# Where the first Fourier step's result is read, and the order of the first loads of the output stage

## The chip, the cores and the metric

The kernel runs on one core of one Trainium2 chip. The metric is the time of one execution on the device in microseconds (us), and lower is better. The profile is one execution recorded by the hardware. In it, PE is the matrix engine (TensorE), DVE the vector engine, ACT the scalar engine, POOL is GpSimd and SP is the engine that issues most of the DMAs.

## What is computed

One layer of a hybrid diffusion backbone, for 4096 grid tokens (64 x 64) and 256 prompt tokens, with width 1024. One input projection feeds four groups of heads (A: neighbourhood attention, B: short convolution, C: Fourier mixing, D: gated linear attention), each is multiplied by its gate, and one output projection merges them. The change is about group C and the output projection:

```python
def fourier_mix(u):
    b, s, w = u.shape
    ug = u.reshape(b, s, N_FOURIER, w // N_FOURIER).astype(jnp.float32)
    f = jnp.fft.fftn(ug, axes=(1, 3), norm='ortho').real
    return f.reshape(b, s, w).astype(u.dtype)
...
    yC = fourier_mix(uC) * jax.nn.silu(gC)
    oD, s_f, s_b = gla_mixer(qD, kD, vD, aF, aB, up_f, b_f, up_b, b_b, s0_f, s0_b, gn_l)
    yD = oD * jax.nn.silu(gD)
    y = jnp.concatenate([yA, yB, yC, yD], axis=-1) @ w_out_l
    return x + gate * y, k, v, s_f, s_b
```

## The kernel before

The program is six stages, one behind the other: modulation, two projection stages (0 and 1), attention with the linear-attention scan, the Fourier stage, and the output stage. Each ends with a wait for its last stores and a barrier of all engines, so nothing of a stage starts before the one ahead of it has ended. Inside a stage every engine runs its own list, written out by hand, and semaphores tie the lists together. There is no scheduler: the order in the code is the order on each engine, and each engine's DMAs go into one queue in that order.

The transform over the 4096 positions is done in two steps of 64. The first runs inside projection stage 1 (`first_step` on PE): for each tile of 128 tokens (two grid columns), real and imaginary results land in `y_sb` (partitions 0 to 63 real, 64 to 127 imaginary), and `send_columns` on SP writes them into the scratch tensor `y1`, 2 x 64 x 64 x 256 numbers, 8.4 MB. The second step is the Fourier stage. SP reads `y1` back in 8 groups of 8 frequencies `k1` (`mid`, 1 MB each, as two DMAs of 64 partitions) and beside each group 256 KB of the table `second`. PE multiplies (L1539, two results of 64 rows side by side), ACT and DVE copy the banks out into one of four buffers `yx`, and ACT stores them into `yc` (L1557, two DMAs of 64 partitions for each group). Group i can be copied out only when the stores of group i - 4 have landed. The prompt's own transform (L1528, tables `whole` and `g` loaded by POOL) stands ahead of all this on PE, and its copy and store (L1546, L1548) ahead of it on ACT.

The attention stage takes 34 tiles of 128 queries (0 to 31 grid, 32 and 33 prompt). In the list of SP tile i begins, when tile i - 1 is done on PE, with the loads for tile i + 1: four of values (L1051), then the scan's (`scan` L1057, `kv` L1059), then queries or keys for a later block; it ends with the stores of tile i (`ya`) and of tile i - 1 (`od`). PE needs the scan's loads of a tile at the end of its first head.

The output stage mixes the four groups (`load_mix`: 9 loads; `combine` on DVE, `join` on POOL, `turn` on PE), splits the mixed tile into a high and a low part (`high` on ACT, `low` on DVE), and multiplies it by the output weights, which come in 8 pieces of 512 KB (`stage_w`, four buffers) and are split in the same way (L1718 on ACT, L1795 on DVE). Pieces 0 to 3 are the weights of the left half of the columns, 4 to 7 of the right. The product of a half waits for its pieces:

```python
for h in range(2):
    pe.wait_ge(gated, t * 2 + h + 1)
    pe.wait_ge(w_lo_done, (h + 1) * len(PIECES) // 2)
    ...
    product(pe, ps_y[s][h][:, :], ...)
    if h == 0:
        prepare_next(turn, t, s)
```

## Time and profile before

| | |
|---|---|
| median of 3 runs | 2787.53 us (2783.85 to 2796.4) |
| profiled execution, its own time | 2787.69 us |
| its span (first to last instruction) | 2786.0 us |
| PE busy | 2554.9 us, 92% of the span |
| DVE, ACT, POOL busy | 45%, 36%, 27% |
| attention stage, last DMAs issued | until 2268.1 us |
| Fourier stage, first DMA | 2270.76 us |
| output stage, first DMA | 2335.51 us |

A busy share is an average over stages. PE is near full in the two projection stages and in most of the output stage, and has almost nothing to do between 2265 and 2368 us, so a gain or loss there shows fully in the time. Times named below are from the start of the span.

### The profile page before, as it was taken

The page shows a single profiled execution, that of the slowest core. Times are in us where ns is not written, and L with a number is a line of the kernel's source. Part 1 is how long each engine was busy: PE and PEld are TensorE (multiplying, and loading weights), DVE is VectorE, ACT ScalarE, POOL GpSimd, SP SyncE. Part 2 cuts the span into 40 slices and gives each one's busy share as a digit, 9 for nine tenths or more (in the row PEclk, how much of TensorE's full clock was granted, in tenths as well). Part 3 has the DMA queues.
Part 4 walks back from the last instruction along what each step waited for, and adds up shares of the span by engine and source line. Part 5 has one row for each costly group of instructions (what it writes and reads, how often), then busy time and mean ns, then how long its engine had stood idle before and what let it go on. Part 6 is the DMA issues. An engine that isn't in the chain of part 4 may idle for free. (4 is left out here: it accounts for less than half of the span.)

```text
span 2786.0 us, 53595 instructions
## 1 busy us (share of the span) xinstructions
PE 2554.9 (92%) x19228; PEld 2056.2 (74%) x19228; DVE 1257.1 (45%) x2620; ACT 990.5 (36%) x2031; POOL 740.5 (27%) x1145
## 2 busy tenths in 40 slices
PE   3899999999999949999999997999899952999999
PEld 1788888888888838888888875777777741888887
DVE  2444343443443343323323325667667722566555
ACT  2444444444444342222222214555555621111110
POOL 2223233233332310000000004333233321444442
PEclk8999999999999979999999998999999976999999
DMA  7433333333333254223223218887677667766664
GB/s 289 144 106 119 110 114 122 102 118 118 107 119 107 84 184 140 93 81 96 92 81 97 92 52 170 179 180 170 144 154 168 153 151 235 244 202 213 209 203 135
DMA packets 271822, 395.35 MB, mean 142 GB/s; under 512 B 43270, under 2 KB 192678, under 8 KB 269628
## 3 DMA queue, kind: packets, MB, share of 16 engines
q1 hardware_dynamic: 258396, 368.21, 46.3%
q10 hardware_dynamic: 12735, 24.07, 2.5%
q8 instruction: 96, 1.57, 0.3%
q0 software_dynamic: 544, 1.09, 0.2%
q14 instruction: 51, 0.41, 0.1%
HBM read 267.31 MB, written 125.96 MB: 141 GB/s over the span
## 5 line engine op out<-in xcount | busy, mean ns | idle before, releaser
L258 PE MATMUL p_ps_m<-p_w_hi,p_h_hi 128*128 128x512 f32 x1904 | 771.8, 405 | 21.1 <-DVE p_h_lo L823 21.1
L260 PE MATMUL p_ps_m<-p_w_hi,p_h_lo 128*128 128x512 f32 x1904 | 750.4, 394 | 0.0
L259 PE MATMUL p_ps_m<-p_w_lo,p_h_hi 128*128 128x512 f32 x1904 | 750.3, 394 | 0.0
L258 PEld LDWEIGHTS p_ps_m<-p_w_hi,p_h_hi 128*128 128x128 f32 x1904 | 359.7, 189 | 99.6 <-issue 21.8
L260 PEld LDWEIGHTS p_ps_m<-p_w_hi,p_h_lo 128*128 128x128 f32 x1904 | 358.9, 189 | 80.7
L259 PEld LDWEIGHTS p_ps_m<-p_w_lo,p_h_hi 128*128 128x128 f32 x1904 | 360.1, 189 | 73.3
L258 PE MATMUL o_ps_y<-o_w_hi,o_y_hi 128*128 128x512 f32 x544 | 217.5, 400 | 9.7 <-DVE o_y_lo L1784 9.7
L260 PE MATMUL o_ps_y<-o_w_hi,o_y_lo 128*128 128x512 f32 x544 | 217.4, 400 | 0.0
L259 PE MATMUL o_ps_y<-o_w_lo,o_y_hi 128*128 128x512 f32 x544 | 215.7, 397 | 0.0
L537 POOL TENSOR_TENSOR p_ve<-p_ss,p_eps 128x1 f32<-128x1 f32 x68 | 12.9, 190 | 601.1 <-ACT p_xr L603 601.1
L814 DVE TENSOR_TENSOR p_xt<-p_xt,p_ps_r 128x1024 f32<-128x1024 f32 x68 | 82.7, 1216 | 193.0 <-PE p_ps_r L714 193.0
L577 POOL TENSOR_TENSOR p_la<-p_la,p_cum 128x512 f32<-128x512 f32 x34 | 44.0, 1295 | 426.7 <-ACT p_cum L616 426.7
L817 DVE TENSOR_SCALAR p_xt<-p_xt,mod 128x128 f32<-128x128 f32 x544 | 146.1, 342 | 2.5
L1463 DVE COPY a_p_t<-a_ps_t 128x512 f32<-128x512 f32 (+1 forms) x136 | 91.6, 674 | 117.0 <-PE a_ps_t L1309 117.0
L1710 ACT ACTIVATE o_y_hi<-o_ps_t 128x512 fp32r<-128x512 f32 x68 | 36.9, 596 | 257.5 <-PE o_ps_t L1739 257.5
L823 DVE TENSOR_TENSOR p_h_lo<-p_xt,p_h_hi 128x1024 fp32r<-128x1024 f32 x68 | 83.3, 1225 | 98.7 <-ACT p_h_hi L608 98.7
L258 PEld LDWEIGHTS o_ps_y<-o_w_hi,o_y_hi 128*128 128x128 f32 x544 | 102.9, 189 | 33.3 <-issue 10.1
L259 PEld LDWEIGHTS o_ps_y<-o_w_lo,o_y_hi 128*128 128x128 f32 x544 | 102.8, 189 | 24.9
L260 PEld LDWEIGHTS o_ps_y<-o_w_hi,o_y_lo 128*128 128x128 f32 x544 | 102.7, 189 | 23.8
L1345 PEld LDWEIGHTS a_ps_o<-a_v_win,a_p_t 128*64 128x64 f32 x2112 | 75.3, 140 | 57.9 <-issue 41.2
L1345 PE MATMUL a_ps_o<-a_cv,a_p_t 128*64 128x64 f32 x2048 | 92.0, 226 | 23.5 <-DMA a_kv<-s_kv 16.1
L1414 DVE TENSOR_REDUCE a_max_c<-a_ps_c 128x1 f32<-128x512 f32 x128 | 88.0, 687 | 47.4 <-PE a_ps_c L1288 46.1
(217 smaller groups left out, 4512.6 us busy)
## 6 DMA issues: line engine op xcount, KB each, us to landing
a_scan<-s_scan SPq DMA_DIRECT2D x68, 258.0 KB, 5.7
s_scan<-p_w_raw SPq DMA_DIRECT2D x136, 128.0 KB, 2.4
a_kv<-s_kv SPq DMA_DIRECT2D x68, 256.0 KB, 6.3
a_v_win<-s_p SPq DMA_DIRECT2D x132, 128.0 KB
p_xr<-in_x_sample SPq DMA_DIRECT2D x32, 512.0 KB, 4.0
p_xt<-in_x_sample_t SPq DMA_DIRECT2D x32, 512.0 KB, 4.7
p_xr<-in_x_columns SPq DMA_DIRECT2D x32, 512.0 KB, 10.1
p_xt<-in_x_columns_t SPq DMA_DIRECT2D x32, 512.0 KB, 10.8
```

The costliest lines, as they stand in the source:

```text
L258: pe.matmul(out, left_hi(k), right_hi(k), start=(k == 0), stop=False)
L259: pe.matmul(out, left_hi(k), right_lo(k), start=False, stop=False)
L260: last = pe.matmul(out, left_lo(k), right_hi(k), start=False, stop=(k == K8 - 1))
L537: pool.tensor_tensor(ve[s][:, :], ss[s][:, :], eps[:, 0:1], ALU.add).then_inc(ve_done, 1)
L577: pool.tensor_tensor(la[:, :, :], la[:, :, :], cum[:, :, :], ALU.subtract).then_inc(la_done, 1)
L814: dve.tensor_tensor(xt[s][:, :, :], xt[s][:, :, :], ps_r[:, s, :].unsqueeze(1).broadcast_to([P, K8, P]), ALU.mult).then_inc(normed, 1)
L817: last = dve.tensor_scalar(xt[s][:, k, :], xt[s][:, k, :], keep["mod"][:, 1, k, j:j + 1], keep["mod"][:, 0, k, j:j + 1], ALU.mult, ALU.add)
L823: dve.tensor_tensor(h_lo[s][:, :, :], xt[s][:, :, :], h_hi[s][:, :, :], ALU.subtract).then_inc(lo_done, 1)
L1345: last = pe.matmul(ps_o[z * HD:z * HD + HD, at:at + HD], p_t[p][:, m * P + z * HD:m * P + z * HD + HD], val, start=(n == 0), stop=(n == le ...
L1414: dve.tensor_reduce(max_c[:, p:p + 1], ps_c[p][:, :], AX.X, ALU.max).then_inc(maxc_done, 1)
L1463: dve.tensor_copy(p_t[p][:, 0:cols], ps_t[0][:, 0:cols]).then_inc(t0_sb, 1)
L1710: act.activation(y_hi[s][:, 4 * b:4 * b + 4, :], ps_t[b][:, :, :], ACT.Copy).then_inc(hi_done, 1)
```

## The change

Five edits.

1. `y1` is laid out by group: (8, 2, 64, 8, 256), so that a group of 8 frequencies is one block of 1 MB. `send_columns` issues four DMAs for each tile in place of two.
2. The table `second` (2 MB) and the first four groups of `mid` (4 MB) have buffers that live through the attention and the Fourier stage. SP loads the groups there in tiles 26 to 29 and the table in tile 30, behind the stores of the tile.
3. The Fourier stage loads groups 4 to 7 alone, each in one DMA of 128 partitions.
4. The prompt's transform stands behind the groups on PE and on ACT.
5. In the output stage SP loads the input of tile 0, weight pieces 0 to 3, the input of tile 1, then pieces 4 to 7; the split of the pieces on ACT and DVE is put in the matching order; `taps` and `gn` go to ACT's queue.

```diff
             def send_columns(t, s):
                 sp.wait_ge(y_done, t + 1)
                 for r in range(2):
-                    sp.dma_start(io["y1"][r, bass.ds(2 * t, 2)].rearrange("b k c -> k b c"), y_sb[s][64 * r:64 * r + 64, :, :]).then_inc(y_sent[s], 16)
+                    for z in range(2):
+                        sp.dma_start(io["y1"][:, r, bass.ds(2 * t, 2)][:, z], y_sb[s][64 * r:64 * r + 64, z, :]).then_inc(y_sent[s], 16)
...
-                            act.wait_ge(y_sent[1 - s], (t - 2) * 16 + (1 - s) * -16 + 16)
+                            act.wait_ge(y_sent[1 - s], (t - 2 + s) * 32)
...
+                if isinstance(i, int) and 26 <= i < 30:
+                    g = i - 26
+                    sp.dma_start(fourier["mid"][:, 8 * g:8 * g + 8, :], io["y1"][g].rearrange("r b q c -> (r b) q c")).then_inc(fourier_in, 16)
+                if isinstance(i, int) and i == 30:
+                    sp.dma_start(fourier["second"][:, :, :], io["dft_second"]).then_inc(fourier_in, 16)
...
-            for i in range(GROUPS):
-                for r in range(2):
-                    sp.dma_start(mid[64 * r:64 * r + 64, 8 * i:8 * i + 8, :], io["y1"][r, :, 8 * i:8 * i + 8, :]).then_inc(group_in[i], 16)
-                sp.dma_start(second[:, 8 * i:8 * i + 8, :], io["dft_second"][:, 8 * i:8 * i + 8, :]).then_inc(group_in[i], 16)
+            for i in range(GROUPS // 2, GROUPS):
+                at = 8 * i - 32
+                sp.dma_start(mid[1][:, at:at + 8, :], io["y1"][i].rearrange("r b q c -> (r b) q c")).then_inc(group_in[i], 16)
...
+            for n in range(2 * GROUPS):
+                if n % 2 == 0 and n >= GROUPS:
+                    pe.wait_ge(group_in[n // 2], 16)
+                if n >= BANKS:
+                    pe.wait_ge(freed[n % 2], (n - BANKS) // 2 + 1)
+                ...
             pe.wait_ge(gp_in, 64)
...
-            load_mix(1, 1)
-            sp.dma_start(taps[:, :, :].rearrange("p a c -> p (a c)"),
-                         io["conv_w"].rearrange("a t c -> a (t c)").broadcast_to([P, 3 * W_GRP])).then_inc(taps_in, 16)
...
+            load_mix(0, 0)
+            load_weights(range(4))
+            load_mix(1, 1)
+            load_weights(range(4, 8))
...
             square(0, 0)
+            split_high(range(2))
+            high(0, 0, 0)
+            split_high(range(2, 4))
             square(1, 1)
+            split_high(range(4, 8))
...
             combine(0, 0)
+            split_low(range(2))
+            low(0, 0, 0)
+            split_low(range(2, 4))
             combine(1, 1)
+            split_low(range(4, 8))
```

Three places show how the lists move. The first is SP in the attention stage, at the end of tile 26 and in the loads for tile 28 (`s_y` is the scratch tensor `y1`, `s_p` holds the values). Before:

```order
L1031 DMA a_k_lo<-s_qk_lo 128x2x960
L1116 DMA s_ya<-a_o_sb 8x16x256
L1121 DMA s_od<-a_od_sb 128x256 x2
L1051 DMA a_v_win<-s_p 128x1x256 x4
L1057 DMA a_scan<-s_scan 64x1032
L1059 DMA a_kv_0<-s_kv 64x2x512
```

Of the change:

```order
L1033 DMA a_k_lo<-s_qk_lo 128x2x960
L1118 DMA s_ya<-a_o_sb 8x16x256
L1123 DMA s_od<-a_od_sb 128x256 x2
L1126 DMA f_mid<-s_y 128x2048
L1053 DMA a_v_win<-s_p 128x1x256 x4
L1059 DMA a_scan<-s_scan 64x1032
L1061 DMA a_kv_0<-s_kv 64x2x512
```

One DMA of 1 MB stands ahead of all loads for tile 28, and in the same way in the next three tiles; in tile 30 it is the table of 2 MB.

The second is SP at the start of the output stage. Before:

```order
L1636 DMA o_u<-s_conv_u 128x256 x3
L1641 DMA o_taps<-in_conv_w 128x768
L1646 DMA o_stage_w<-in_w_out 128x2x512 x8
L1649 DMA o_gate<-s_mod 128x1024 x2
```

Of the change (its two stretches of inputs end with the `o_u` rows):

```order
L1643 DMA o_u<-s_conv_u 128x256 x3
L1650 DMA o_stage_w<-in_w_out 128x2x512 x4
L1636 DMA o_ya<-s_ya 128x256
...
L1643 DMA o_u<-s_conv_u 128x256 x3
L1650 DMA o_stage_w<-in_w_out 128x2x512 x4
L1658 DMA o_gate<-s_mod 128x1024 x2
```

`taps` has left SP's list, and four weight pieces have moved ahead of the input of tile 1.

The third is DVE at the same place, before:

```order
L1778 TENSOR_TENSOR o_o_n<-o_o,o_r 128x256
L1769 TENSOR_TENSOR o_o<-o_od 128x256
L1771 TENSOR_TENSOR o_u_w<-o_u,o_taps 128x768
L1773 TENSOR_REDUCE o_ss<-o_o_sq 128x4
L1776 TENSOR_REDUCE o_conv<-o_u_w 128x256
L1778 TENSOR_TENSOR o_o_n<-o_o,o_r 128x256
L1795 TENSOR_TENSOR o_w_lo<-o_stage_w,o_w_hi 128x2x512 x4
L1784 TENSOR_TENSOR o_y_lo<-o_ps_t,o_y_hi 128x512 x2
L1795 TENSOR_TENSOR o_w_lo<-o_stage_w,o_w_hi 128x2x512 x4
```

Of the change:

```order
L1795 TENSOR_TENSOR o_o_n<-o_o,o_r 128x256
L1809 TENSOR_TENSOR o_w_lo<-o_stage_w,o_w_hi 128x2x512 x2
L1801 TENSOR_TENSOR o_y_lo<-o_ps_t,o_y_hi 128x512 x2
L1809 TENSOR_TENSOR o_w_lo<-o_stage_w,o_w_hi 128x2x512 x2
L1786 TENSOR_TENSOR o_o<-o_od 128x256
L1788 TENSOR_TENSOR o_u_w<-o_u,o_taps 128x768
L1790 TENSOR_REDUCE o_ss<-o_o_sq 128x4
L1793 TENSOR_REDUCE o_conv<-o_u_w 128x256
L1795 TENSOR_TENSOR o_o_n<-o_o,o_r 128x256
L1809 TENSOR_TENSOR o_w_lo<-o_stage_w,o_w_hi 128x2x512 x4
```

The whole `combine` of tile 1 (five operations) has moved from ahead of the first four pieces to behind them, and now stands ahead of the last four.

## Rows read from the trace of the kernel before

**Rows 1.** The page's first line.

```profile
span 2786.0 us, 53595 instructions
```

**Rows 2.** Chain of work that ended last (start us, us, what).

```profile
2344.42 6.87 DMA o_taps<-in_conv_w
...
2400.68 0.87 PE o_ps_t L1739 x8
...
2412.76 0.87 PE o_ps_t L1739 x8
```

**Rows 3.** Windows of the Fourier stage: PE, PEld, DVE, ACT, POOL, PEclk, DMA share, GB/s.

```profile
2271.00:2288.00 17.00, 0.00 (x0) 0.00 (x0) 0.00 (x0) 0.00 (x0) 2.98 (x4) 0.50 0.97 224
2313.00:2334.00 21.00, 9.44 (x48) 4.55 (x48) 2.77 (x4) 2.39 (x4) 0.00 (x0) 0.71 0.83 269
```

**Rows 4.** DMA view of 2265 to 2336 us: packets; issues, KB each, us to landing.

```profile
DMA packets 5271, 16.53 MB, mean 233 GB/s; under 512 B 1312, under 2 KB 1941, under 8 KB 4245
...
f_mid<-s_y SPq DMA_DIRECT2D x16, 512.0 KB, 22.1
s_yc<-f_yx ACTq DMA_DIRECT2D x16, 256.0 KB, 12.4
```

**Rows 5.** Timeline of the Fourier stage (start, us, engine, line; idle before and releaser).

```profile
2270.76 1.16 SPq L1510 DMA_DIRECT2D f_mid<-s_y  x2
...
2288.57 6.56 PE L1528 MATMUL f_psp<-f_gp,f_whole 128*128 128x256 f32 x16 [23.32 <-DMA f_whole<-in_dft_whole]
...
2313.62 0.60 ACT L1544 ACTIVATE f_yx<-f_ps 128x512 f32<-128x512 f32 x1 [10.34 <-DMA s_yc<-f_yx]
...
2315.13 3.47 PE L1539 MATMUL f_ps<-f_mid,f_second 128*64 128x256 f32 x16 [3.40 <-DMA f_second<-in_dft_second]
...
2327.37 2.63 PE L1539 MATMUL f_ps<-f_mid,f_second 128*64 128x256 f32 x16 [2.76 <-DMA f_second<-in_dft_second]
...
2335.51 0.34 SPq L1638 DMA_DIRECT2D o_gn<-in_gla_norm_g  x1
```

**Rows 6.** Windows with DMAs of 64 and of 128 partitions, columns as in rows 3.

```profile
2172.00:2174.00 2.00, 2.00 (x34) 1.73 (x30) 1.52 (x7) 1.12 (x3) 0.00 (x0) 1.00 1.12 199
2375.00:2377.00 2.00, 2.00 (x15) 1.74 (x14) 0.00 (x0) 0.56 (x2) 0.00 (x0) 1.00 1.07 391
```

**Rows 7.** Attention: SP issues and PE tile ends in the timeline.

```profile
2165.24 3.86 SPq L1051 DMA_DIRECT2D a_v_win<-s_p  x4
...
2171.64 0.60 SPq L1059 DMA_DIRECT2D a_kv<-s_kv  x1
...
2178.72 1.10 PE L1373 MATMUL a_ps_g<-a_kv,a_scan 128*64 128x64 f32 x32
...
2240.74 1.13 PE L1373 MATMUL a_ps_g<-a_kv,a_scan 128*64 128x64 f32 x32
```

**Rows 8.** Attention windows behind two bursts of loads, columns as in rows 3.

```profile
2176.00:2178.00 2.00, 1.90 (x20) 1.17 (x20) 1.80 (x6) 1.82 (x4) 2.00 (x5) 1.00 0.42 99
2236.00:2238.00 2.00, 1.77 (x36) 1.52 (x37) 1.33 (x5) 1.30 (x4) 1.23 (x2) 1.00 0.03 9
```

**Rows 9.** The stores of `y1`: their issues; waits of SP in projection stage 1.

```profile
L438 SPq DMA_DIRECT2D s_y<-p_y_sb x64: 612/630/670, 1055.4 to 1644.0; - x64
...
SPq L438 <- ACT p_y_sb L693: 209.6, 22, 11.1
```

**Rows 10.** Timeline of the output stage's start, as in rows 5.

```profile
2343.47 0.72 POOL L1672 TENSOR_TENSOR o_mix<-o_ya,o_g_ad 128x256 f32<-128x256 f32 x1 [7.82 <-DMA o_u<-s_conv_u]
...
2354.38 0.94 DVE L1778 TENSOR_TENSOR o_o_n<-o_o,o_r 128x256 f32<-128x256 f32 x1 [0.50 <-POOL o_r L1680]
...
2361.24 5.15 DVE L1795 TENSOR_TENSOR o_w_lo<-o_stage_w,o_w_hi 128x1024 fp32r<-128x1024 f32 x4
...
2367.86 0.77 PE L258 MATMUL o_ps_y<-o_w_hi,o_y_hi 128*128 128x512 f32 x1 [9.71 <-DVE o_y_lo L1784]
...
2375.80 1.03 PE L1739 MATMUL o_ps_t<-ident,o_mix 128*128 128x128 f32 x8
...
2382.12 0.69 DVE L1807 TENSOR_TENSOR o_gx<-o_ps_y,o_gate 128x512 f32<-128x512 f32 x1 [3.77 <-DMA o_x<-in_x_sample]
...
2388.38 1.09 PE L1739 MATMUL o_ps_t<-ident,o_mix 128*128 128x128 f32 x8 [0.35 <-POOL o_mix L1685]
```

More of the change, by code:

```diff
@@ L1484, in fourier_stage @@
         sem = lambda name: new_sem("f_" + name)
-        second = sb("second", [P, 64, 64])
-        mid = sb("mid", [P, 64, W_GRP])
+        second = early["second"]
+        mid = [early["mid"], sb("mid1", [P, 32, W_GRP])]
         yx = [sb(f"yx{s}", [P, 4, W_GRP]) for s in range(SLOTS)]
@@ L1523, in _ @@
         def _(pe):
+            for n in range(2 * GROUPS):
[3 more added lines that the diff above has]
+                    pe.wait_ge(freed[n % 2], (n - BANKS) // 2 + 1)
+                for j in range(2):
+                    for z in range(2):
+                        k1 = 8 * (n // 2) + 4 * z + n % 2 * 2 + j
+                        last = pe.matmul(ps[n % BANKS][64 * z:64 * z + 64, j, :], second[:, k1, :], mid[k1 // 32][:, k1 % 32, :], start=True, stop=True)
+                last.then_inc(filled, 1)
             pe.wait_ge(gp_in, 64)
@@ L1530, in _ @@
             last.then_inc(yp_mm, 1)
-            for n in range(2 * GROUPS):
-                if n % 2 == 0:
-                    pe.wait_ge(group_in[n // 2], 48)
-                if n >= BANKS:
-                    pe.wait_ge(freed[n % 2], (n - BANKS) // 2 + 1)
-                for j in range(2):
-                    for z in range(2):
-                        k1 = 8 * (n // 2) + 4 * z + n % 2 * 2 + j
-                        last = pe.matmul(ps[n % BANKS][64 * z:64 * z + 64, j, :], second[:, k1, :], mid[:, k1, :], start=True, stop=True)
-                last.then_inc(filled, 1)
         @block.scalar
@@ L1694, in _ @@
         def _(act):
+            act.dma_start(taps[:, :, :].rearrange("p a c -> p (a c)"),
+                          io["conv_w"].rearrange("a t c -> a (t c)").broadcast_to([P, 3 * W_GRP])).then_inc(taps_in, 16)
+            act.dma_start(gn[:, :], io["gla_norm_g"].broadcast_to([P, HD])).then_inc(gn_in, 16)
             for s in range(2):
@@ L1710, in high, with split_high @@
                     act.activation(y_hi[s][:, 4 * b:4 * b + 4, :], ps_t[b][:, :, :], ACT.Copy).then_inc(hi_done, 1)
+            def split_high(which):
+                for n in which:
+                    h, m = PIECES[n]
+                    act.wait_ge(w_in[n % 4], 16 * (n // 4 + 1))
+                    act.activation(w_hi[:, 2 * m:2 * m + 2, 512 * h:512 * h + 512], stage_w[n % 4][:, :, :], ACT.Copy).then_inc(w_hi_done, 1)
             square(0, 0)
+            split_high(range(2))
+            high(0, 0, 0)
+            split_high(range(2, 4))
             square(1, 1)
-            for n, (h, m) in enumerate(PIECES):
-                if n == len(PIECES) // 2:
-                    high(0, 0, 0)
-                act.wait_ge(w_in[n % 4], 16 * (n // 4 + 1))
-                act.activation(w_hi[:, 2 * m:2 * m + 2, 512 * h:512 * h + 512], stage_w[n % 4][:, :, :], ACT.Copy).then_inc(w_hi_done, 1)
+            split_high(range(4, 8))
             for t, s, j in tile_pairs(act):
@@ L1785, in low, with split_low @@
                                       ALU.subtract).then_inc(lo_done, 1)
+            def split_low(which):
+                for n in which:
+                    h, m = PIECES[n]
+                    part = slice(2 * m, 2 * m + 2), slice(512 * h, 512 * h + 512)
+                    dve.wait_ge(w_hi_done, n + 1)
+                    dve.tensor_tensor(w_lo[:, part[0], part[1]], stage_w[n % 4][:, :, :], w_hi[:, part[0], part[1]],
+                                      ALU.subtract).then_inc(w_lo_done, 1)
             dve.wait_ge(taps_in, 16)
             combine(0, 0)
+            split_low(range(2))
+            low(0, 0, 0)
+            split_low(range(2, 4))
             combine(1, 1)
[L1790 to L1796 removed]
+            split_low(range(4, 8))
             dve.wait_ge(small_in, 32)
@@ L1824, in build @@
             projection_stage(nc, io, keep, 1, early)
-            attention_scan_stage(nc, io, keep, early)
-        fourier_stage(nc, io, keep)
+            fourier = {"second": inner.enter_context(nc.sbuf_tensor("f_second", [P, 64, 64], F32)),
+                       "mid": inner.enter_context(nc.sbuf_tensor("f_mid0", [P, 32, W_GRP], F32))}
+            attention_scan_stage(nc, io, keep, early, fourier)
+            fourier_stage(nc, io, keep, fourier)
         output_stage(nc, io, keep)
```

40 lines of the change are left out of this document (18 added, 22 removed).

## The prediction

> **What bounds the kernel now.** I read the page first, then the stretches in which PE has little to do. The span is 2786.0 us [rows 1]; the same execution took 2787.69 us, so 1.7 us lie outside it, and the median of the runs is 2787.53, so the sum can be made against 2787.7. The chain of waits shows that the end is set by PE through the output stage, at one tile each 12.08 us (2412.76 - 2400.68) [rows 2], and before that by DMAs and by the preparation of the output stage. Two stretches are therefore worth their full length: the Fourier stage, 64.75 us (2270.76 to 2335.51), in which PE is only fed by loads [rows 5], and the 32.35 us from there to the first output product at 2367.86 [rows 10].
>
> In the Fourier stage the DMA engines are the bound. While nothing but loads run they are busy 0.97 and move 224 GB/s, later with stores mixed in 269 GB/s [rows 3]. Over the whole stretch 16.53 MB move at 233 GB/s [rows 4]. PE waits 23.32 us for the prompt's table, then for each group again; the last group comes at 2327.37, and the stage ends 8.1 us behind it [rows 5].
>
> In the output stage the inputs of tile 0 are there at 2343.47 (POOL starts on them), but DVE needs `taps`, which stands behind the inputs of tile 1 on SP and lands 6.87 us after its issue at 2344.42, at 2351.3 [rows 2, 10]. Then DVE does both combines, four weight pieces (5.15 us from 2361.24) and the low part, and the first product starts [rows 10].
>
> **The change, part by part.**
>
> *Stores of y1.* Two more issues for each of 32 tiles, at 0.63 us each [rows 9]: 1.3 us of SP for a tile. SP stands waiting for ACT at this very store, 209.6 us over 22 tiles, 9.5 each [rows 9], so the cover is there and I cost it at 0. Were the cover gone it would be 32 x 1.3 = 40 us. The reader of the buffer's semaphore comes two tiles later.
>
> The Trainium skill's page "DMA: Bandwidth & Descriptors", section "Why a DMA increments its semaphore by 16 and not by 1", says that a DMA uses the largest number of engines up to 16 that divides the outermost size on both sides; the new store has 8 groups outermost in memory, so by that rule it runs on 8 engines, not 16. By the rule 64 KB would take about twice as long, still far less than two tiles; it changes no term, but it speaks against this layout and is part of the rival that ends slower.
>
> *Loads in the attention stage.* 1 MB in each of tiles 26 to 29, 2.1 MB in tile 30, ahead of the loads for the tile after next. The nearest rates are 199 GB/s in a burst of DMAs of 64 partitions and 391 GB/s where all have 128 [rows 6]: 1.05 MB takes 2.7 to 5.3 us, 2.1 MB takes 5.4 to 10.5 us. What is behind them: the values and scan loads, issued from 2165.24 to 2172.2 [rows 7]. They have landed by about 2176.5: the DMA share has fallen to 0.42 in the window from 2176 [rows 8]. PE ends its tile at 2178.72 + 1.1 and wants the scan's inputs some 3 us into the next, about 2183. The slack is 6 us, more than 5.3, so 0 for these four tiles. For the 2.1 MB: in the window from 2236 the loads are done (share 0.03) [rows 8], the tile ends at 2240.74 + 1.1 [rows 7], need about 2245: slack 8.5 to 9 against 5.4 to 10.5. I put 1 us on the path, with 0 below and 8 above (an excess of 1.5 in each of five tiles).
>
> *Fourier stage.* Of its loads, 4.2 MB of `mid` and 2.1 MB of table go. Left are 4.19 MB of `mid` (4 DMAs), 1.05 MB for the prompt, 4.19 MB of stores and 0.26 MB of the prompt's result: 9.7 MB of 16.0. The rate is the unknown. Bounds: at the 233 GB/s of before it takes 41.6 us [rows 4], at the 391 of full DMAs 24.8 us [rows 6]. The loads are now 128 partitions each, the stores still 64, so I take the middle, 310 to 330: 30 us. Two things are added to that. At the front PE can start at once from the buffers, but the store of group 0 cannot be issued before one group (3.47 us slow clock [rows 5]) and its copy; loads fill that time, so 1.5 us for the first packet only. At the end, behind the last load, stand the group's product (2.63), now the prompt's product (6.56 at the granted clock of 0.5, half of it at full clock; taken 5), then its copy (0.6), issue (0.4), landing and barrier: before, from the last group to the next stage was 8.1 us [rows 5]; now it is 8.1 + 5 = 13, of which 4.5 are stores that count in the 30. So 1.5 + 30 + 8.5 = 40 us, against 64.75: **-25 us**. With the bounds of the rate: 24.8 + 10 = 35 (-30), 41.6 + 10 = 52 (-13). The wait for a free `yx` slot, 10.34 us before [rows 5], lies inside this: stores can only be made when the engines serve them.
>
> The Trainium skill's page "SBUF — State Buffer", section "Can I just issue two DMAs to hit both halves?", says no: only one transfer over all 128 partitions reaches all ports, and two halves serialize. The trace agrees with its sign (199 against 391 [rows 6]). By that rule alone the loads would run at the full rate, and the stage would lie near the 35 us end.
>
> *Output stage.* From its start S, in the steps of before. Inputs of tile 0 are in at S + 7.6 (before: 2343.47 - 2335.51 = 8.0, with `gn` ahead). `taps` comes on ACT's queue with the first issues and is there. DVE's combine took 4.0 us (2351.3 to 2355.3) [rows 10]; POOL's own three products now run beside it and not ahead, +0.5: S + 12.1. Then two pieces at 1.29 (5.15 / 4): S + 14.7. `turn` (2 us slow) starts at S + 13, ACT's high parts end by S + 15.5, DVE's low parts by S + 16.2. Two more pieces: S + 19. The four pieces are 2.1 MB, issued by S + 6.2 and landed by about S + 14 at 300 GB/s, in time. **The first product starts at S + 19 in place of S + 32.35.** But the second product needs all 8 pieces, and DVE stands with the combine of tile 1 (4.3) and four pieces (5.15) ahead: S + 19 + 9.5 = S + 28.5. PE is at that point itself at S + 19 + 7.9 (2375.80 - 2367.86) + 1 = S + 28, so it waits 0.5. Before, the second product started at 2376.8, S + 41.3. Gain there: 41.3 - 28.5 = 12.8. What is late next: `x` of tile 0. Before it came at 2382.12, just in time (PE waited 0.35 at 2388.38 for the mix of tile 2 that hangs on it) [rows 10]. It is still behind pieces, gates and the inputs of tile 2 on SP; the gap between the last piece and `x` stays about 10 us, which makes it some 1 us later against PE. **-12 us**, bounds -14 (no wait at all) and -3 (the last four pieces, which now wait for a buffer to be split before they can be issued, land late and only the `taps` wait is gone in part).
>
> **Sum:** 2787.7 + 0 + 1 - 25 - 12 = **2752 us** (2751.7).
>
> **Rivals.**
> - *Only bytes are saved, not rate:* the Fourier stage runs on at 233 GB/s and takes 52 us. For it: DMA share was 0.97 with 224 GB/s [rows 3]. Against it: 391 GB/s with full DMAs [rows 6]. 2787.7 + 1 - 13 - 12 = 2764.
> - *Full rate and no late `x`:* Fourier -30, output -14: 2745. For it: the same 391. Against it: stores of 64 partitions share the engines.
> - *The attention stage pays:* each of the five extra loads stalls PE by 3 us, the rest as forecast: 2787.7 + 15 - 37 = 2766. Against it: 6 us of slack in [rows 7, 8]. In favour: landing is read from a share in windows of 2 us.
> - *The split order fails:* the second product waits for pieces 4 to 7, the output stage gains 3, the rest as forecast: 2761.
> - *Slower:* the stores of `y1`, four per tile with 8 separate blocks in memory, land so late that ACT's copy of the result waits for its buffer and PE behind it. The tile there is about 19 us (the 9.5 of waiting are half of it), the buffer is free for two tiles, so a store would have to take over 35 us; from there each further us costs 32 us in half the tiles' pairs, 16 or so in all. It decides from 37 us on path: a landing of 38 us, for 2787.7 - 36 + 48 = 2800. Nothing in [rows 9] supports it.
>
> **How the numbers follow.** A difference under 0.5% (14 us) can't be told from none here. Chances: forecast 0.45; bytes only 0.15; full rate 0.18; attention pays 0.09; split order 0.08; slower 0.02; the remaining 0.03 for something unseen of which most would leave the time within 0.5%. The range from 2739 to 2767 takes in the first five. Faster: 0.95; within 0.5%: 0.03; slower: 0.02.
>
> **What would show it.** Right: the Fourier stage's PE work begins within 1 us of its start, its windows show over 300 GB/s, and it lasts about 40 us; the tile ends of PE in the attention stage stay 15 to 16 us apart in tiles 27 to 31; the first output product comes at S + 19, the second half at S + 28 to 29. Wrong: a wait of PE for `kv` or `scan` in tiles 28 to 32, a wait for a `yx` slot that outlasts the loads, a first output product late because of the weight loads, or a tile in projection stage 1 that is longer than before.

## The result, and the profile after

The changed kernel takes 2751.24 us (median of 4 runs, 2742.02 to 2755.03), the kernel before 2786.98 us on the same chip: a ratio of 0.9865, with a 95% interval of 0.9839 to 0.9891. The forecast was 2752. The profiled execution took 2755.03 us with a span of 2753.3, 32.7 less than the 2786.0 of before [rows 1]. Read by stages, from the first DMA of one to the first DMA of the next:

| | before | after | difference | forecast |
|---|---|---|---|---|
| start to the Fourier stage | 2270.76 | 2282.43 | +11.7 | +1 |
| Fourier stage | 64.75 | 29.88 | -34.9 | -25 |
| output stage | 450.5 | 441.0 | -9.5 | -12 |
| span | 2786.0 | 2753.3 | -32.7 | -36 |

So the total came out, and none of its three stage terms did. The timeline of the changed kernel's Fourier stage (start, us, engine, line; idle before and releaser):

```profile
2282.43 2.24 SPq L1518 DMA_DIRECT2D f_mid<-s_y  x4
2282.46 13.29 PE L1539 MATMUL f_ps<-f_mid,f_second 128*64 128x256 f32 x96 [5.62 <-PEq L81]
...
2297.30 1.95 PE L1539 MATMUL f_ps<-f_mid,f_second 128*64 128x256 f32 x16 [1.55 <-DMA f_mid<-s_y]
2298.56 0.60 ACT L1551 ACTIVATE f_yx<-f_ps 128x512 f32<-128x512 f32 x1 [5.33 <-DMA s_yc<-f_yx]
2301.33 3.42 PE L1539 MATMUL f_ps<-f_mid,f_second 128*64 128x256 f32 x16 [2.08 <-DMA f_mid<-s_y]
2304.68 3.88 PE L1545 MATMUL f_psp<-f_gp,f_whole 128*128 128x256 f32 x16
2309.23 0.42 ACTq L1564 DMA_DIRECT2D s_yc<-f_yp  x1
2312.31 0.33 SPq L1636 DMA_DIRECT2D o_ya<-s_ya  x1
```

The 23.32 us in which PE waited for the prompt's table [rows 5] are gone: PE starts with the stage, waits 3.6 us in all for its last two groups, and the last one is there 18.9 us behind the stage's start (2301.33 - 2282.43) in place of 56.6. The wait for a free `yx` slot is 5.33 us, not 10.34 [rows 5]. The DMA view of the stage, and behind it windows (columns as in rows 3, in the order of this sentence) of the middle of the stage and of two places in the attention stage:

```profile
DMA packets 2449, 9.72 MB, mean 313 GB/s; under 512 B 400, under 2 KB 656, under 8 KB 1936
...
f_mid<-s_y SPq DMA_DIRECT2D x4, 1024.0 KB, 8.4
s_yc<-f_yx ACTq DMA_DIRECT2D x16, 256.0 KB, 7.4
```

```profile
2286.00:2302.00 16.00, 12.37 (x104) 8.00 (x102) 3.62 (x6) 2.56 (x5) 0.00 (x0) 0.93 1.01 400
2252.00:2254.00 2.00, 0.89 (x18) 0.69 (x20) 1.67 (x4) 0.26 (x2) 0.00 (x0) 0.96 0.90 230
2254.00:2256.00 2.00, 2.00 (x31) 1.56 (x27) 0.00 (x0) 0.50 (x3) 0.00 (x0) 0.50 1.04 213
```

At the same DMA share (1.01 against 0.97) the engines now move 400 GB/s where they moved 224 [rows 3]. The last two windows belong to the attention stage: there the granted clock falls from 0.96 to 0.50, which is 1.2 of 2.4 GHz, behind a window in which PE was busy 0.89 of 2 us. In the attention stage's timeline, SP's issues in tile 26, and then ends of tiles and waits on PE:

```profile
2167.18 0.45 SPq L1126 DMA_DIRECT2D f_mid<-s_y  x1
2167.74 4.78 SPq L1053 DMA_DIRECT2D a_v_win<-s_p  x4
...
2176.77 0.60 SPq L1061 DMA_DIRECT2D a_kv<-s_kv  x1
...
2181.45 1.10 PE L1381 MATMUL a_ps_g<-a_kv,a_scan 128*64 128x64 f32 x32
2186.11 0.34 PE L1353 MATMUL a_ps_o<-a_cv,a_p_t 128*64 128x64 f32 x4 [0.61 <-DMA a_kv<-s_kv]
2202.58 0.34 PE L1353 MATMUL a_ps_o<-a_cv,a_p_t 128*64 128x64 f32 x4 [0.66 <-DMA a_kv<-s_kv]
2219.29 0.34 PE L1353 MATMUL a_ps_o<-a_cv,a_p_t 128*64 128x64 f32 x4 [0.90 <-DMA a_kv<-s_kv]
...
2247.02 0.75 PE L1381 MATMUL a_ps_g<-a_kv,a_scan 128*64 128x64 f32 x18
...
2274.86 1.98 PE L1381 MATMUL a_ps_g<-a_kv,a_scan 128*64 128x64 f32 x32 [0.54 <-DVE a_s_at L1451]
```

The four tiles from 2178.72 to 2240.74 [rows 7] took 62.0 us; from 2181.45 to 2247.02 they take 65.6, with a wait for the scan's `kv` in each of three of them that no tile in the profile of before has. These waits add up to 2.2 us of the 3.6 (1.2 of 2.9 in changed_again); PE's own work is 0.9 us longer, the rest lies in small gaps, and neither was followed further. The last two take 27.8 us, not 22.5. On SP the loads behind the new one are stretched: the values' four issues take 4.78 us, not 3.86, and from the first of them to the last `kv` it is 9.0 us (2176.77 - 2167.74) where it was 6.4 (2171.64 - 2165.24) [rows 7]. Between 2150 and 2240 us a load of `kv` takes 9.5 us from issue to landing (median), 6.2 before. The start of the output stage:

```profile
2321.92 0.43 DVE L1786 TENSOR_TENSOR o_o<-o_od 128x256 f32<-128x256 f32 x1 [16.43 <-DMA o_u<-s_conv_u]
2326.33 0.94 DVE L1795 TENSOR_TENSOR o_o_n<-o_o,o_r 128x256 f32<-128x256 f32 x1 [1.31 <-POOL o_r L1689]
2327.20 2.88 DVE L1809 TENSOR_TENSOR o_w_lo<-o_stage_w,o_w_hi 128x1024 fp32r<-128x1024 f32 x2
...
2335.26 0.76 PE L258 MATMUL o_ps_y<-o_w_hi,o_y_hi 128*128 128x512 f32 x1 [4.25 <-DVE o_w_lo L1809]
2338.94 5.17 DVE L1809 TENSOR_TENSOR o_w_lo<-o_stage_w,o_w_hi 128x1024 fp32r<-128x1024 f32 x4
2344.25 0.47 PE L258 MATMUL o_ps_y<-o_w_hi,o_y_hi 128*128 128x512 f32 x1 [0.49 <-DVE o_w_lo L1809]
```

From the stage's start S = 2312.31 the inputs of tile 0 are in at S + 9.6, the first product starts at S + 22.95 and the second at S + 31.9, which before was S + 41.3. The 9.4 us between these are the stage's gain.

### The profile page after: what moved, and what is told of

Its sections match the earlier page's. It is cut to its first block and busy times, and to the rows that moved or that the text cites. A ratio compares the mean times of both kernels' runs of the same rounds, so it can differ in the third digit from the quotient of the medians.

```text
span 2753.3 us, 53748 instructions
## 1 busy us (share of the span) xinstructions
PE 2558.0 (93%) x19228; PEld 2060.3 (75%) x19228; DVE 1256.9 (46%) x2620; ACT 989.7 (36%) x2031; POOL 740.0 (27%) x1145
## 5 line engine op out<-in xcount | busy, mean ns | idle before, releaser
L258 PE MATMUL p_ps_m<-p_w_hi,p_h_hi 128*128 128x512 f32 x1904 | 771.6, 405 | 20.5 <-DVE p_h_lo L824 20.4
L260 PEld LDWEIGHTS o_ps_y<-o_w_hi,o_y_lo 128*128 128x128 f32 x544 | 102.6, 189 | 23.8
## 6 DMA issues: line engine op xcount, KB each, us to landing
p_xr<-in_x_columns SPq DMA_DIRECT2D x32, 512.0 KB, 10.2
```

The costliest lines, as they stand in the source:

```text
L258: pe.matmul(out, left_hi(k), right_hi(k), start=(k == 0), stop=False)
L260: last = pe.matmul(out, left_lo(k), right_hi(k), start=False, stop=(k == K8 - 1))
```

## The experiments

The theory after this reading: the loads of the Fourier stage became fast because they span 128 partitions, not because of the new layout; the early loads cost the attention stage more than forecast because they meet its own loads. All ratios below are to the kernel before on the same chip. A summary by stage, in us, from the profile of each kernel ("four tiles" and "last two" are the attention tiles named above):

| kernel | median | ratio (95%) | four tiles | last two | Fourier | output |
|---|---|---|---|---|---|---|
| before | | | 62.0 | 22.5 | 64.75 | 450.5 |
| changed | 2751.24 | 0.9865 (0.9839-0.9891) | 65.6 | 27.8 | 29.88 | 441.0 |
| changed_again | 2743.58 | 0.9849 (0.9827-0.9870) | 64.9 | 25.7 | 29.61 | 441.6 |
| no_early | 2758.89 | 0.9907 (0.9884-0.9929) | 62.0 | 22.5 | 50.08 | 441.6 |
| half_loads | 2749.63 | 0.9875 (0.9852-0.9899) | 65.2 | 27.8 | 37.24 | 441.2 |
| old_layout | 2745.44 | 0.9861 (0.9840-0.9882) | 65.3 | 28.0 | 29.78 | 441.3 |
| one_dma | 2766.77 | 0.9935 (0.9914-0.9956) | 62.1 | 26.1 | 44.58 | 449.9 |
| late_issue | 2750.91 | 0.9879 (0.9859-0.9900) | 71.6 | 25.5 | 29.63 | 442.3 |
| last_tiles | 2740.74 | 0.9841 (0.9819-0.9863) | 62.1 | 26.1 | 29.48 | 441.4 |
| prompt_first | 2759.59 | 0.9915 (0.9888-0.9943) | 65.5 | 26.1 | 41.34 | 441.5 |
| out_only | 2774.12 | 0.9968 (0.9950-0.9985) | 62.1 | 26.0 | 62.88 | 441.4 |
| taps_only | 2784.83 | 0.9993 (0.9978-1.0009) | 62.1 | 22.5 | 63.84 | 446.4 |
| taps_behind | 2744.57 | 0.9864 (0.9842-0.9886) | 62.1 | 22.5 | 29.56 | 441.9 |
| best | 2741.42 | 0.9843 (0.9823-0.9864) | 62.1 | 22.5 | 29.28 | 441.3 |

**changed_again**: the changed kernel with no edit.

> The changed kernel once more, unchanged, as the measure of how far two profiles and two medians of one kernel lie apart. Theory: Fourier stage 29.9 us and output stage 441.0 us within 0.5 us of the first profile, a median within 3 us of 2751; the tiles 26 to 33 of the attention stage together again 8 to 13 us longer than the 127.1 to 129.3 us of the kernels without early loads. Rival, that the 10 us are chance of one profile (clock dips): 130 us or less this time.

The Fourier stage repeats to 0.3 us and the output stage to 0.6; the four tiles are long again. From the end of tile 25 to the Fourier stage it is 132.0 us this time, not 137.0: less than the 8 to 13 us extra that was expected, and not down to the 130 of the rival, though one_dma, with nothing loaded early, has 131.5. So this total alone doesn't decide it; the four tiles do. The median is 7.7 us lower, more than the 3 that were expected. What differs lies ahead of the change: the row that ends tile 25 stands at 2145.4 us in the first profile of the changed kernel and at 2136.9 in this one, and in the fourteen profiles of this study, whose code up to there is the same but for the stores of `y1`, anywhere from 2134.6 to 2145.4. A difference of a few us between two medians is therefore decided by stages here, not by totals.

**no_early**: nothing is loaded in the attention stage.

```diff
...
-            for i in range(GROUPS // 2, GROUPS):
-                at = 8 * i - 32
-                sp.dma_start(mid[1][:, at:at + 8, :], ...)
+            for i in range(GROUPS):
+                at = 8 * i % 32
+                sp.dma_start(mid[i // 4][:, at:at + 8, :], ...)
+                sp.dma_start(second[:, 8 * i:8 * i + 8, :], io["dft_second"][:, 8 * i:8 * i + 8, :]).then_inc(group_in[i], 16)
```

> The changed kernel with nothing loaded in the attention stage: all eight groups of the first step's result (one DMA of 128 partitions each) and the table (eight pieces) are loaded in the Fourier stage. Theory, that DMAs of 128 partitions over contiguous blocks run at about 400 GB/s: the stage moves 16 MB, 12 of them loads, and takes 48 to 52 us (64.75 before, 29.9 in the changed kernel); the attention stage goes back to its length of before (-11 us); total near 2764, 0.992 of before. Rival, that only the bytes moved out of the stage helped and the rate stays that of before (233 GB/s, some 270 at best): the stage takes 60 us or more, total 2774 or more.

50.1 us, as the theory has it. The same 16 MB that took 62.9 to 64.75 us now take 50.1, and the attention stage is as long as before (62.0 and 22.5). So of the 34.9 us, 14.7 are there with no byte moved out of the stage (with the new place of the prompt's product, which costs some of it: see one_dma), and the bytes moved out give 20.2 (there the prompt's new place helps: see prompt_first).

**half_loads**: the four late groups as two DMAs each.

```diff
-                sp.dma_start(mid[1][:, at:at + 8, :], io["y1"][i].rearrange("r b q c -> (r b) q c")).then_inc(group_in[i], 16)
+                for r in range(2):
+                    sp.dma_start(mid[1][64 * r:64 * r + 64, at:at + 8, :], io["y1"][i][r]).then_inc(group_in[i], 16)
```

> The changed kernel, but the four groups that are loaded in the Fourier stage come as two DMAs of 64 partitions each, from the same contiguous blocks of 1 MB. Theory, that the number of partitions sets the rate: the 4.2 MB come at about 210 GB/s in place of 400, the last group is 6 to 9 us later, and the stage takes 36 to 39 us in place of 29.9; total +6 to +9. Rival, that the contiguous block made the loads fast: within 2 us of 29.9.

37.2 us, 7.4 more, from contiguous blocks. A window of 16 us in the middle of the stage:

```profile
2270.00:2286.00 16.00, 11.62 (x84) 7.55 (x82) 2.77 (x4) 2.39 (x4) 1.50 (x3) 0.82 1.02 261
```

The engines are busy at 1.02 and move 261 GB/s, against 400 in the changed kernel. A DMA of 64 partitions is also half as large, 512 KB, but the size is not what slows it. In the changed kernel's output stage weight pieces of 512 KB over 128 partitions, with inputs of 128 and 256 KB around them, move at 404 GB/s:

```profile
2320.00:2326.00 6.00, 0.00 (x0) 0.00 (x0) 3.10 (x4) 2.53 (x3) 3.95 (x5) 0.50 1.06 404
```

The median does not show the 7.4 us (2749.63, between the two medians of the changed kernel); it is less than those differ by.

**old_layout**: the changed kernel with `y1` as before, two stores for each tile; only the loads differ from before, and they span 128 partitions.

```diff
-                    for z in range(2):
-                        sp.dma_start(io["y1"][:, r, bass.ds(2 * t, 2)][:, z], y_sb[s][64 * r:64 * r + 64, z, :]).then_inc(y_sent[s], 16)
+                    sp.dma_start(io["y1"][r, bass.ds(2 * t, 2)].rearrange("b k c -> k b c"), y_sb[s][64 * r:64 * r + 64, :, :]).then_inc(y_sent[s], 16)
...
-                sp.dma_start(mid[1][:, at:at + 8, :], io["y1"][i].rearrange(...
+                sp.dma_start(mid[1][:, at:at + 8, :], io["y1"][:, :, 8 * i:8 * i + 8, :].rearrange(...
```

> The changed kernel with the result of the first step stored as in the kernel before (its old shape, two stores for each tile, not four), and each group still loaded by one DMA of 128 partitions, which now reads runs of 8 KB a partition out of 128 places 64 KB apart and not one block of 1 MB. Theory, that the number of partitions sets the rate and the block layout does nothing: Fourier stage within 1 us of 29.7, total within 3 us of the changed kernel. Rival, that the contiguous megabyte in memory is what made the loads fast: the stage is 5 us or more longer.

29.78 us: the theory again. A window of 16 us in it:

```profile
2276.00:2292.00 16.00, 11.41 (x104) 7.60 (x102) 3.72 (x6) 2.66 (x5) 0.19 (x1) 1.00 1.01 406
```

406 GB/s from 8 KB runs that lie 64 KB apart: the block of 1 MB does nothing for the time.

**one_dma**: the kernel before, one line (and the count that PE waits for).

```diff
-                for r in range(2):
-                    sp.dma_start(mid[64 * r:64 * r + 64, 8 * i:8 * i + 8, :], io["y1"][r, :, 8 * i:8 * i + 8, :]).then_inc(group_in[i], 16)
+                sp.dma_start(mid[:, 8 * i:8 * i + 8, :], io["y1"][:, :, 8 * i:8 * i + 8, :].rearrange("r b q c -> (r b) q c")).then_inc(group_in[i], 16)
```

> The kernel before, with the two DMAs of 64 partitions for each group made into one of 128, from the same places of the old layout, and nothing else. Theory (partitions set the rate): the Fourier stage falls from 64.75 (62.9 and 63.8 in two other traces of the same code) to 50 to 54 us, as in the kernel with nothing loaded early (50.1), plus what the prompt's product ahead of the groups costs; total near 2776. Rival (layout sets the rate): within 2 us of 63.

44.58 us, 18.3 to 20.2 less than in the three profiles with two DMAs, and better than expected. A window of 16 us in its Fourier stage, and PE there:

```profile
2278.00:2294.00 16.00, 7.16 (x20) 5.45 (x22) 0.00 (x0) 0.36 (x1) 0.00 (x0) 0.53 1.01 403
```

```profile
2286.84 6.76 PE L1527 MATMUL f_psp<-f_gp,f_whole 128*128 128x256 f32 x16 [18.38 <-DMA f_whole<-in_dft_whole]
2293.53 12.51 PE L1538 MATMUL f_ps<-f_mid,f_second 128*64 128x256 f32 x112
2309.64 3.28 PE L1538 MATMUL f_ps<-f_mid,f_second 128*64 128x256 f32 x16 [3.59 <-DMA f_second<-in_dft_second]
```

Seven groups run through behind the prompt's product without a wait, and the stage ends 8.9 us behind the last one. With the prompt's product last (no_early) the stage takes 5.5 us longer for the same bytes (no_early has the new layout too, which by old_layout does nothing): there PE waits for its first group anyway, and the prompt's product stands exposed at the end.

**prompt_first**: the changed kernel with the prompt's product, copy and store ahead of the groups.

> The changed kernel, but PE and ACT do the prompt's transform ahead of the eight groups again, as before. Theory: PE can't use the buffers filled in the attention stage until the prompt's table has landed (21.8 to 23.3 us in the traces of before, estimated at 10 to 16 with 4.2 MB of other loads in place of 12.6); the first stores of yc leave that much later and come in a crowd, so the stage takes 38 to 42 us in place of 29.9, total +8 to +12. Rival, that the engines are busy with loads in that time anyway and the stage stays bound by its 9.7 MB: within 3 us of 29.9.

41.34 us, as the theory has it. PE waits for the prompt's table 19.81 us and then runs all eight groups in one piece:

```profile
2288.75 6.09 PE L1535 MATMUL f_psp<-f_gp,f_whole 128*128 128x256 f32 x16 [19.81 <-DMA f_whole<-in_dft_whole]
2294.77 14.03 PE L1546 MATMUL f_ps<-f_mid,f_second 128*64 128x256 f32 x128
```

Some 5.6 us of this wait lie ahead of the stage; from its start (2274.54) the table is there at 14.2 us, at 17.8 before. The median is 16 us above that of changed_again on the same chip, of which 4 are the longer attention stage of this profile. So the edit that puts the prompt last is worth 11.6 us when half of the groups lie ready, and costs 5.5 when none do.

**late_issue**: the early loads are issued behind the loads for the next tile.

```diff
+                if isinstance(i, int) and 26 <= i < 30:
+                    ...
                 sp.wait_ge(o_done, 4 * i + 5)
...
-                if isinstance(i, int) and 26 <= i < 30:
-                    ...
```

> The changed kernel, but each of the five early loads is issued behind its tile's own loads (values, scan, queries, keys, bias), not ahead of them. Theory, that the attention stage lost its 10 us because the extra bytes stood ahead of the values and scan inputs in the queue: tiles 27 to 32 go back to 15.6 us, PE's waits for the keys-and-values of the scan are gone, and the attention stage gets 5 to 10 us back, total 2741 to 2746. Rival, that the bytes cost the same wherever they stand (the engines are loaded, or the clock falls anyway): no more than 2 us from the changed kernel, and the Fourier stage may begin with a wait for the table.

The theory on the order in the queue falls: the four tiles take 71.6 us, longer still, and the median is that of the changed kernel. The worst wait, and the windows behind it:

```profile
2182.74 0.34 PE L1353 MATMUL a_ps_o<-a_cv,a_p_t 128*64 128x64 f32 x4 [3.23 <-DMA a_kv<-s_kv]
```

```profile
2180.00:2182.00 2.00, 0.00 (x0) 0.00 (x0) 0.33 (x3) 0.00 (x0) 0.00 (x0) 1.00 0.77 220
2182.00:2184.00 2.00, 1.26 (x22) 1.19 (x24) 0.00 (x0) 0.87 (x3) 1.01 (x2) 0.74 0.26 101
2184.00:2186.00 2.00, 2.00 (x25) 1.88 (x22) 0.00 (x0) 0.11 (x2) 1.06 (x2) 0.50 0.26 88
```

The early groups now take 13.6 us (median) to land, 6.9 in the changed kernel: they share the engines with the tile's own loads and with those of the next tile. Which of the two makes `kv` late was not taken apart. PE does nothing for these 3.23 us, the granted clock then falls to 0.50, and the tile takes 20.4 us.

**last_tiles**: all five early loads in tile 32, behind its own loads.

```diff
-                if isinstance(i, int) and 26 <= i < 30:
-                    g = i - 26
-                    ...
-                if isinstance(i, int) and i == 30:
+                if isinstance(i, int) and i == 32:
+                    for g in range(4):
+                        sp.dma_start(fourier["mid"][:, 8 * g:8 * g + 8, :], ...)
                     sp.dma_start(fourier["second"][:, :, :], io["dft_second"]).then_inc(fourier_in, 16)
```

> The changed kernel, but all five early loads (6.3 MB) are issued in tile 32, behind the last loads that the attention stage needs itself. In the trace of the kernel before the DMA engines stand nearly idle from there to the stage's end, 2250 to 2270. Theory, that the early loads cost the attention stage time because they meet its own loads, in whatever order: tiles 26 to 31 go back to 15.2 to 15.8 us each, no wait for keys-and-values of the scan, from the start of tile 26's end (the row of the scan's result ahead of it) to the Fourier stage 127 to 130 us in place of 137; the 6.3 MB need 16 us at 391 GB/s and are in before the stage ends; total near 2742. Rival, that the stage's tail then waits for these loads or that the stores of the last tiles are held up by them: the stage is as long as in the changed kernel or longer, total 2750 or more.

The four tiles are at 62.1 again with no wait for `kv`, and from the end of tile 25 to the Fourier stage it is 129.6 us, against 137.0 and 132.0 in the two profiles of the changed kernel. Windows of the attention stage's end:

```profile
2246.00:2260.00 14.00, 12.33 (x140) 9.34 (x136) 4.43 (x13) 2.90 (x10) 3.84 (x6) 0.51 1.01 419
2260.00:2268.00 8.00, 1.97 (x32) 1.79 (x32) 0.42 (x1) 0.91 (x2) 0.01 (x1) 0.50 0.36 119
```

6.3 MB go through a stretch in which the engines stood idle before, at 419 GB/s beside PE's work, and are in ahead of the stage's end. They are not free there. The table, last in the queue, takes 18.0 us to land, and the tiles' stores of `od` stand behind it. In this profile the last tile is slow by itself (14.8 us at the low clock) and covers that. In the next two kernels with the same loads (taps_behind, then best) the last tile takes 11.3 us, and ACT's last copy waits for such a store:

```profile
2262.62 0.60 ACT L1253 ACTIVATE a_od_sb<-a_ps_g 128x512 f32<-128x512 f32 x1 [5.08 <-DMA s_od<-a_od_sb]
2268.16 0.60 ACT L1253 ACTIVATE a_od_sb<-a_ps_g 128x512 f32<-128x512 f32 x1 [6.33 <-DMA s_od<-a_od_sb]
```

From the row that ends the last tile to the Fourier stage it is then 10.4 and 11.0 us, against 7.5 to 7.6 in all others. From the end of tile 27 to the Fourier stage the three kernels with the loads in tile 32 take 95.0 to 95.7 us, the five with nothing early 92.0 (three, with 22.5 in the last two tiles) or 95.6 to 95.7 (two, with the clock fallen), and the five with loads ahead of their tiles' own 98.2 to 101.0. So the new place costs some 3 us where the clock holds, and the old one 2.4 to 6 more. The median is 2.8 us below changed_again on the same chip, with intervals of the ratios that overlap (0.9819 to 0.9863 and 0.9827 to 0.9870): the gain is shown in the stage, not in the total.

**out_only**: the kernel before with the output stage of the changed one.

> The kernel before with only the output stage of the changed kernel (taps on ACT's queue, weight pieces in two halves between the inputs of two tiles, new order of the splits). If that stage's gain is its own: -9.5 us as read between the two traces, total 2777, 0.9965 of before, all stages ahead of it unchanged. Rival, that part of the 9.5 came from a different state of the queues at the stage's start (the stores of the Fourier stage and the prompt's store end closer to it now): -12 to -13, since the inputs of tile 0 then land at 7.6 us and not 9.6 us behind the stage's start.

The output stage takes 441.4 us, -9.1: its gain is its own, and the first expectation holds. The inputs of tile 0 land 10.2 us behind the stage's start, here too.

**taps_only**: the kernel before with `taps` and `gn` on ACT's queue, weight pieces and splits as before.

> The kernel before with only the loads of taps and norm weights moved to ACT's queue; weight pieces and splits stay as they were. Theory, that most of the output stage's gain is the wait for taps that is gone: the combine starts 7.5 to 8.5 us behind the stage's start in place of 15.8, and the stage gets 5 to 8 us shorter, total near 2780. Rival, that the order of the splits is what counts and the eight pieces (landed last) set the second product anyway: 0 to 3 us.

-4.1 us, between the two. The combine begins 10.3 us behind the start and not at 8, so the taps are no longer waited for but cost the inputs behind them. The order of the pieces and splits is the other 5.0 us (446.4 to 441.4).

**taps_behind**: last_tiles, with `taps` on SP behind the inputs of tile 0.

```diff
             load_mix(0, 0)
+            sp.dma_start(taps[:, :, :]...).then_inc(taps_in, 16)
             load_weights(range(4))
...
                 dve.wait_ge(conv_done, t + 1)
+                if isinstance(t, int) and t == 0:
+                    dve.wait_ge(taps_in, 16)
```

> The kernel with all early loads in tile 32, and in the output stage taps issued on SP behind the inputs of tile 0 and ahead of the weight pieces, not as the first issue of ACT's queue; DVE waits for taps only ahead of the product that reads them. In all six traces in which taps stands first the combine begins 9.6 to 10.3 us behind the stage's start, with POOL at 8.0 before. Theory, that the 384 KB of taps ahead of tile 0's inputs delay these by about 2 us: POOL and DVE's first operation begin at 7.8 to 8.3 us, taps land at 9.5 to 10.5, and the first product comes at 22 to 23.5 in place of 23.3, the stage is 0 to 1.5 us shorter than 441.4. Rival, that the weight pieces behind are what slows the inputs: 9.6 us or later again.

The stage begins at 2297.73. Its timeline:

```profile
2306.14 0.42 DVE L1785 TENSOR_TENSOR o_o<-o_od 128x256 f32<-128x256 f32 x1 [16.02 <-DMA o_u<-s_conv_u]
2308.37 0.96 DVE L1789 TENSOR_TENSOR o_u_w<-o_u,o_taps 128x768 f32<-128x768 f32 x1 [1.81 <-DMA o_taps<-in_conv_w]
...
2317.67 1.54 POOL L1682 TENSOR_TENSOR o_mix<-o_ya,o_g_ad 128x256 f32<-128x256 f32 x1 [3.90 <-DMA o_u<-s_conv_u]
```

The inputs are in at 8.4 us, not 9.6 to 10.3, so `taps` ahead of them is what delays them. Nothing is won by it: the product with `taps` starts at 10.6, the first output product at 22.7 (23.3 in last_tiles), and the inputs of tile 1, now 3.90 us late for POOL, take it back. The stage is 0.4 us longer.

**best**: last_tiles, with the prompt's product ahead of the last group.

```diff
             for n in range(2 * GROUPS):
+                if n == 2 * GROUPS - 2:
+                    pe.wait_ge(gp_in, 64)
+                    ...
                 if n % 2 == 0 and n >= GROUPS:
```

The line that is left out is the prompt's product; ACT copies and stores it ahead of the last group too.

> The kernel with all early loads in tile 32, and the prompt's product moved from behind the last group to ahead of it, into PE's wait for that group (0.82 and 2.33 us ahead of the last two groups in the trace of that kernel). Theory: the prompt's copy and store no longer stand behind the last group's, so the Fourier stage takes 27 to 28.5 us in place of 29.5, total near 2739, 0.983 of before. Rival, that the prompt's table has not landed by then or that ACT, which waits for the prompt's product, frees the buffers of the last groups later: 29.5 us or more.

29.28 us, no gain of size: the rival holds, the table lands only 17.35 us behind the stage's start.

```profile
2291.07 3.72 PE L1536 MATMUL f_psp<-f_gp,f_whole 128*128 128x256 f32 x16 [1.70 <-DMA f_whole<-in_dft_whole]
```

PE waits for it and the last group waits behind it. No version stands clearly apart from last_tiles.

## Why the prediction came out

**Stores of y1: 0, right.** From the first to the last of these stores it is 589.9 and 590.0 us in the two profiles of the changed kernel, 588.6 in those of before and of old_layout, and the 1.3 us are the two more issues of the last tile alone. old_layout takes the two more away again and is within 3 us of the changed kernel's second median. How long such a store takes to land no row here shows, so the rule of the Trainium skill's page "DMA: Bandwidth & Descriptors", section "Why a DMA increments its semaphore by 16 and not by 1", stays unchecked; the rival that ended slower did not come.

**Attention: +1 forecast, +11.7 read, some 6 of it from the change.** The step that failed is "the slack is 6 us, more than 5.3, so 0 for these four tiles". The landing was read from a DMA share of 0.42 in a window of 2 us, and the transfer was taken as the only thing the new load costs. In fact the loads behind it are issued over 9.0 us, not 6.4, and a `kv` takes 9.5 us to land, not 6.2: counted from the end of tile 26, the last `kv` is issued 12.5 us behind it, not 8.7 (2176.77 - 2164.27 and 2171.64 - 2162.92), and lands 3.3 us later still. That is 7.1 us against the 6 of slack, and 2176.77 + 9.5 = 2186.3 is where PE's first wait for it ends (2186.11). The forecast added only the 5.3 us of the transfer at its worst and called the slack enough. A wait for `kv` appears in tiles where none was; I had named it as what would show me wrong. (One profile without early loads, out_only, has such a wait too, 0.87 us in tile 27; none of the eight has one in the four tiles.) In the five profiles with early loads in tiles 26 to 30 ahead of the tiles' own the four tiles take 64.9 to 65.6 us, in the eight without them 62.0 to 62.1: 3.2 us on average. The last two tiles take 25.7 to 28.0 with them (five) and 22.5 to 26.1 without (eight): that is where the granted clock falls, and it falls ahead of the last tile (25.7 us or more) in all five of the first kind and in three of the eight of the other. On average it is 3.2 us more (27.1 against 23.8). So 6.4 us is the reading for the change, of which the half in the last two tiles is the weaker one: it rests on how often the clock falls, in thirteen profiles. Of the 11.7, the pair of profiles has 8.9 in these six tiles, 1.7 by the end of tile 25 and 1.0 in tiles 26 and 27, these last two figures no more than the spread of profiles of one code. The 6.4 is inside the bound of 8 that I gave, whose "excess of 1.5 in each of five tiles" is close to the truth in sum; I took the wrong end.

**Fourier stage: -25 forecast, -34.9 read.** Right were the rate's direction, the immediate start of PE and the choice of 128 partitions as the cause. Mis-sized were two terms. The rate while loads run is 400 GB/s, not 310 to 330: stores of 64 partitions among loads of 128 do not pull it down to the middle. The tail was forecast at 13 us behind the last load, with 4.5 of it stores; it is 11.0. And I put all 9.7 MB ahead of the tail but for those 4.5 us, though loads are not queued behind stores: from the start to the last load it was to be 1.5 + 25.5 = 27 us and it is 18.9. 27 + 13 = 40; 18.9 + 11.0 = 29.9. The lower bound of 35 us, which had the full rate but the same tail arithmetic, was no bound. Seen over the whole stage, tail and all, the mean is 325 GB/s (9.72 MB in 29.88 us), the very middle that I took: the 30 us were right for the whole stage, and the 10 us beside them were too much. The slow bound was misread as well. The 233 GB/s [rows 4] are the mean of a window of 71 us, 6 of them outside the stage; over the stage itself it was 247 GB/s, which makes the 41.6 us 39.3. And PE is not quite as idle around it as the text ahead of the prediction has it: between 2265 and 2368 us it was busy 29.1 of 103 us, with work that stood behind loads.

The rule of the Trainium skill's page "SBUF — State Buffer", section "Can I just issue two DMAs to hit both halves?", that only one transfer over 128 partitions reaches all ports, is what half_loads, old_layout and one_dma test, and they agree with it: 261 against 400 and 406 GB/s. By that rule alone the stage lay near my bound; I should have taken it, since the nearest row of before said the same [rows 6]. The prediction named this and still took the middle.

**Output stage: -12 forecast, -9.5 read.** The order of events is the one forecast, with x late as named (DVE waits 3.99 us for it, nothing hangs on that). The step that failed is "inputs of tile 0 are in at S + 7.6", with `taps` "there" at no cost: its 384 KB go first and the inputs come at S + 9.6 to 10.3 in all eleven profiles with `taps` first. taps_behind shows the cause. The combine also takes 5.3 us, not 4.5: with POOL at work beside it the product with `taps` takes 1.48 us, not 0.95, and the last step waits 1.31 us for POOL's `o_r`, not 0.50. The first product is 4.0 us later than forecast (2.0 for the inputs, 0.8 for the combine, the rest in the splits and the low part), the second 3.4, and 12.8 - 3.4 is 9.4.

**The sum.** +10.7, -9.9 and +2.5 against the terms as forecast leave +3.3 us in the profile, less than the 7.7 by which two medians of the changed kernel differ. That the total fell on the forecast is luck: the attention stage cost more than forecast by about as much as the Fourier stage gained more. "The attention stage pays" (in part, some 6 us and not 15) and "full rate" both came true at once, which my list of rivals held only apart. With what differs from profile to profile taken out, the terms are about +6, -34 (from 62.9 to 64.75 down to 29.6 to 29.9) and -9.1: 2750.

## What to carry to other kernels

When a buffer is loaded as two halves of the partitions, look first whether one DMA over all 128 can read the same places: here one changed line gives nearly half of the gain (one_dma, -17 us in the median), and a new layout of the data gives nothing on top. Move a load out of a stage that is bound by loads into a stretch where the DMA share is near 0, even if it is a late one, rather than in equal parts into tiles that load something of their own: the same 6.3 MB cost 3.2 us in four tiles whose engines looked half idle (and some 3 more in the last two), and some 3 us when they were issued behind the last load of the stage. Look there at what stands behind the moved loads in the same queue: here it was the stage's last stores. The loads in another queue, or behind these stores, were not tried. And where two orders are possible, price the order against what is ready at that moment: putting the prompt last is worth 11.6 us with half the groups ready and costs 5.5 us with none.

## What the runs showed of the hardware

A DMA share near 1 does not say that the engines are at their rate: at a share of 0.97 to 1.02 they moved 224 GB/s (loads, most of the bytes in DMAs of 64 partitions, rows 3), 261 (half_loads, beside stores) and 400 to 419 (loads of 128 partitions, beside stores or alone: the changed kernel, one_dma, old_layout and last_tiles). The Trainium skill's page "SBUF — State Buffer", section "The DMA setup-cost knee (why "@ 1 MiB" ≠ asymptote)", measures a single DMA of 1 MB at about 330 to 340 GB/s; with several in flight these traces show 400 to 419, more than the page's single DMA.

A short wait can cost more than itself: in late_issue PE waited 3.23 us, the granted clock went from 1.00 to 0.50, and the tile took 20.4 us in place of 15.6. In several profiles, of before too, one of the tiles 26 and 27 took 17 to 20 us; in that of before the clock stood at 0.75 in the 6 us from 2148, behind a gap of PE of 1.91 us for which the profile names no releaser. Where this falls differs from run to run of one program and was not settled; how much it has to do with the 11 us by which profiles of the same code differ at the end of tile 25 was not measured.
